# Adding expert outputs in memory by the scatter, and loading small vectors another way

## The chip, the cores and the metric

The kernel runs on one core of a Trainium2 chip. The core has TensorE (PE, matrix products), VectorE (DVE), ScalarE (ACT), GpSimd (POOL) and SyncE (SP, which here only issues DMAs), 16 DMA engines that all queues share, an on-chip memory (SBUF) of 128 partitions and an accumulator memory (PSUM) of 8 banks. The metric is device time in microseconds: 929.48 us, the median of 3 runs from 927.88 to 931.46. The profile is of one further execution.

## What is computed

One layer of a trunk over 256 prompt tokens and 32 sample tokens (288 in all, width 1024), everything in float32. The part before the experts is adaLN modulation from two conditioning vectors, an RMS norm, one input projection, a linear attention with a state, a softmax attention with a cache, an output projection and a second norm. Cut to what matters for the change:

```python
sh1, sc1, gt1, sh2, sc2, gt2 = ada_modulation(c, w_ada, b_ada)     # silu(c) @ w_ada + b_ada, in six parts
h = rms_norm(x, g_mix) * (1.0 + sc1) + sh1
mix, ... = token_mixer(h, ...)                                     # h @ w_in first
x = x + gt1 * mix
h = rms_norm(x, g_ffn) * (1.0 + sc2) + sh2
idx, wts = route(h, w_router, b_router)                            # 8 of 64 experts for each token
routed = sum over the 8 experts e of a token of
         wts * ((silu(h @ w_gate[e]) * (h @ w_up[e])) @ w_down[e])
x = x + gt2 * (routed + shared)
y = rms_norm(x, g_final)
```

So each of 288 tokens gets 8 expert outputs (2304 rows of 4 KB), which must be added.

## The kernel before

All engines run programs written out by hand, with semaphores between them. No scheduler moves anything: the order on an engine is the order in which its block of code is written.

**Head.** SP loads the tokens and eight pieces of `w_ada` of 1 MB (L412, into `ring`), then `w_in` in pieces of 2 MB (into `pair`). PE transposes the tokens, sums their squares (L830) and multiplies the conditioning vectors by the eight pieces (L840). The result stands in PSUM in four pairs of rows. ACT copies them to SBUF (`ada_row`, L491, four copies), PE transposes them (L848, `ada_T`), and DVE makes the modulation (L1255). With it ACT writes the modulated tokens (`hhi`, L507) from the normed ones. ACT also writes the high part of each weight group (`split_hi`, L500, `whi`), DVE the low part (L1274, `wlo`), and from these PE runs the 24 column blocks of the input projection (L870, "z matmuls"). On ACT's own queue, between the norm's square root (L476) and `ada_rows`, stand 12 issues of DMAs: nine small vectors and narrow weights (L479), the cached forget values (`pastf`, L480) and the linear attention's state (L482).

**Expert loop.** A table orders the 64 experts in 32 pairs. A block is up to 64 tokens of each expert of a pair (128 slots on the 128 partitions: expert 0 of the pair on partitions 0 to 63, expert 1 on 64 to 127). A pair mostly takes one block; five further blocks make it 37. The loop's order spreads the pairs with two blocks. In a block PE does the slots' row numbers and weights (L1166), gate and up (L1174), the gather of the next block's tokens (L1150, L1157), and down (L1193). DVE and ACT copy the 128 outputs to `y_slot` (L1607, L641). POOL scatters them (L809): an indirect DMA writes each slot's row of 4 KB to row `rank * 288 + token` of the DRAM tensor `y_d` (eight rows for each token), and empty slots, whose row number lies beyond the bounds, are skipped. POOL waits until it has landed (L812, semaphore `y_gone`). DVE waits for `y_gone` before it computes the next row numbers (`row_f`, L1602, and L1605), and PE waits for these (`row_ok`) at the start of the next block. A scatter issued after one block must therefore have landed before the end of the next. SP loads the weights for the pair after next (L426, `expert_w`, six DMAs of 1 MB each pair): gate and up once PE has read the old ones, down at the end of the pair's last block. PE waits for all six before it starts a block.

**End.** When the last scatter has landed, SP reads `y_d` back: eight loads of 128 KB for the sample tokens (L450) and eight of 1 MB for the prompt tokens (L454) into `y_rank`. The 8 rows of a token are added in part on PE (L1218 with the matrix `four`, L1226 with the identity, accumulating in PSUM) and in part on DVE (L1642 to L1650), which also multiplies by gt2 and adds the rest (`base_tok`, made by ACT at L651). ACT takes the sum of squares and its root (L655, L657), DVE scales (L1629), and SP writes the outputs (L458), in the order sample, first prompt tile, second prompt tile.

Of the kernel before, what the change touches and what calls it, by code (L numbers as in the profile page):

```python
# [53 lines left out]
def layer(nc, x_prompt, x_sample, state_gla, cache_fox_k, cache_fox_v, cache_fox_logf, c_prompt, c_sample,  # L54
# [166 lines left out]
    four = sb("four", [P, NS_])  # L221
# [5 lines left out]
    y_rank = [sb_at(f"y_rank{i}", [P, TOPK, D], F32, RING + 4 * TOPK * D * i) for i in range(3)]  # L227
# [5 lines left out]
    y_d = nc.dram_tensor("y_d", [TOPK * N, D], F32, kind="Internal").ap()  # L233
    gt2_d = nc.dram_tensor("gt2_d", [2, D], F32, kind="Internal").ap()

    def sem(name):
# [8 lines left out]
        "dn_ps acc_ok h2t_ps h2hi_ok h2lo_ok pos_ps rank_ok order_ps table_ok iota_ok rt_zeros sel_ok slots_ps ws_ok row_f_ok row_ok xs_ps xs_ok xg_ps xg_ok pgu_ps sl_ok hid_ok hidT_ps hidT_ok yl_ps yd_ps y_act y_dve y_out y_gone y_rows ys_ps fin_ok sqsum_ok gt2_out tail_in four_ok base_ps base_ok y_sum ssqT_ok rstdT_ok y_ok out_done").split()}  # L245
# [18 lines left out]
    for n, (_, w) in enumerate(pieces):  # L264
        assert w == 1 or at % 2 == 0
        sl = [(at + i) % FRONT for i in range(w)]
        at += w
        waits_of.append(max([owner[q] for q in sl if q in owner], default=-1))
        for q in sl:
            owner[q] = n  # L270
        slots_of.append(sl)
        loads[sl[0]] += 1
        turn.append(loads[sl[0]])
# [6 lines left out]
    def piece_in(eng, n):  # L280

        eng.wait_ge(ring_in[slots_of[n][0]], 16 * turn[n])
# [3 lines left out]

    SHARED = FRONT
# [98 lines left out]
    def ranks_in(i, q):  # L386

        return ring_in[4 * i + q], 16 * (loads[4 * i + q] + PAIRS // 2)
# [10 lines left out]
    def _(sp):  # L399
        for i, (src, tn) in enumerate(((x_prompt[0, 0:128], 128), (x_prompt[0, 128:256], 128), (x_sample[0], 32))):  # L400
            sp.dma_start(x_tok[0:tn, i, :], src).then_inc(s["x_in"], 16)
        for n, (src, w) in enumerate(pieces):
# [9 lines left out]
            sp.dma_start(dst, src).then_inc(ring_in[slots_of[n][0]], 16)  # L412
# [36 lines left out]
        for q in range(TOPK):  # L449
            sp.dma_start(y_rank[2][NS_ * (q % 4):NS_ * (q % 4) + NS_, q // 4, :], y_d[N * q + NP_:N * q + N]).then_inc(ranks_in(2, 0)[0], 16)  # L450
        for i in range(2):
            for q in (2, 3, 0, 1):
                src = y_d.rearrange("(r t) d -> t r d", r=TOPK)[P * i:P * i + P, 2 * q:2 * q + 2, :]
                sp.dma_start(y_rank[i][:, 2 * q:2 * q + 2, :], src).then_inc(ranks_in(i, q)[0], 16)  # L454
        for m, i in enumerate((2, 0, 1)):
            dst = y_sample[0] if i == 2 else y_prompt[0, 128 * i:128 * i + 128]
            sp.wait_ge(s["y_ok"], m + 1)
            sp.dma_start(dst, y_rank[i][0:TN[i], 4, :]).then_inc(s["out_done"], 16)  # L458
# [4 lines left out]
    def _(act):  # L463
# [13 lines left out]
        with nc.allow_non_contiguous_dma(reason="vectors of a few hundred elements"):  # L477
            for dst, src in small[3:]:
                act.dma_start(dst, src).then_inc(s["small_in"], 16)  # L479
        act.dma_start(pastf[:, :, :], cache_fox_logf[0, 0].rearrange("(j p) h -> p j h", p=P)).then_inc(s["cache_in"], 16)  # L480
        for c in range(2):
            act.dma_start(states[:, 4, c, :], state_gla[0, 0, 2 * c:2 * c + 2].rearrange("h k v -> (h k) v")).then_inc(s["state_in"], 16)  # L482

        def ada_rows(r, b):
# [5 lines left out]
            for j in range(4):  # L490
# [4 lines left out]
        def split_hi(g):  # L495

            piece_in(act, FIRST_WIN + g // 2)
# [154 lines left out]
        for m, i in enumerate((2, 0, 1)):  # L652
            n = TN[i]
            act.wait_ge(s["y_sum"], m + 1)
            act.activation(y_rank[i][0:n, 5, :], y_rank[i][0:n, 0, :], ACT.Square, accum_out=ssqT[0:n, i:i + 1]).then_inc(s["ssqT_ok"], 1)  # L655
# [5 lines left out]
    def _(pool):  # L661
# [27 lines left out]
        pool.wait_ge(s["consts"], 1)  # L689
        pool.memset(qA[FD:FD + 2, :, :], 1.0).then_inc(s["ones_ok"], 1)  # L690
# [5 lines left out]
        pool.memset(ada_row[:, :], 0.0).then_inc(s["row_zeros"], 1)  # L696
        pool.wait_ge(s["row_zeros"], 1)
# [86 lines left out]
        pool.tensor_tensor(four[:, :], ident[:, 0:NS_], ident[:, NS_:2 * NS_], ALU.add).then_inc(s["four_ok"], 1)  # L784
        for q in (2, 3):
            pool.wait_ge(s["four_ok"], q - 1)
# [895 lines left out]
```

## Time and profile before

| What | Value |
|---|---|
| Time, median of 3 runs | 929.48 us (927.88 to 931.46) |
| Time of the profiled execution | 932.22 us |
| Its span, first to last instruction | 930.4 us |
| TensorE busy, and its granted clock | 860.4 us (92%), 0.952 of full speed |
| DVE, ACT, POOL busy | 29%, 27%, 10% |
| Read from HBM, written to HBM | 261.34 MB, 22.07 MB |
| Share of 16 DMA engines: SP's queue, POOL's, ACT's | 68.3%, 3.6%, 1.1% |
| Chain that ended last | PE 85%, DVE 5%, DMA 4% |

The page gives shares over the whole span. The three stages that the change touches are the head (0 to 49 us), the expert loop (327 to 883 us) and the end (883 us on). They are read by the chain of waits, which runs back from the last instruction, and by the timeline. A row of the timeline has the start, the duration (of the whole merged run of equal instructions), the engine, the line, and in brackets how long the engine was idle before and what ended that.

### The profile page before, as it was taken

Reading aid. Unit: us, or ns where it says so; the run is one execution under the profiler, and the core shown is the slowest. Engines: PE = TensorE matmul, PEld = TensorE weight load, DVE = VectorE, ACT = ScalarE, POOL = GpSimd, SP = SyncE. Lnnn points to the kernel's source line nnn. Section 1 sums busy time; section 2 is a strip of 40 time slices with the busy share of each in tenths; the row PEclk is TensorE's granted clock in tenths of the full one; section 3 lists DMA queues with packets and bytes.
Section 4 is the critical chain, followed back from the end, with each engine's and each line's share of the span. In section 5 each row is a group of like instructions: output and inputs, shape, how many; then the busy total and the mean of one; then the engine's idle time right before and its main releaser. Section 6 shows DMA issues by size and latency. Waiting matters only on the chain.

```text
span 930.4 us, 13928 instructions
## 1 busy us (share of the span) xinstructions
PE 860.4 (92%) x4436; PEld 470.1 (51%) x4437; DVE 268.6 (29%) x797; ACT 247.9 (27%) x484; POOL 88.4 (10%) x189
## 2 busy tenths in 40 slices
PE   7699999797898999999999999999999999999962
PEld 3199983534686744444444444444444444444521
DVE  2354426435226611111211121121212112121118
ACT  2353424134113312131222212121222213121231
POOL 3000011200022000101101010101101010100000
PEclk9889989798798999999999999999999999999977
DMA  8934447452526369099995999699996999999183
GB/s 326 362 133 160 182 181 276 151 181 92 222 81 263 103 272 376 40 366 415 428 425 245 406 427 426 271 371 420 427 425 254 397 427 426 426 427 426 77 302 157
DMA packets 55370, 273.84 MB, mean 294 GB/s; under 512 B 12720, under 2 KB 13056, under 8 KB 27312
## 3 DMA queue, kind: packets, MB, share of 16 engines
q1 hardware_dynamic: 42064, 258.23, 68.3%
q0 software_dynamic: 6560, 12.55, 3.6%
q10 hardware_dynamic: 6720, 2.70, 1.1%
q8 instruction: 17, 0.28, 0.1%
q14 instruction: 9, 0.07, 0.0%
HBM read 261.34 MB, written 22.07 MB: 305 GB/s over the span
## 4 chain that ended last, share of the span: by engine, by line
PE 85%; DVE 5%; DMA 4%; ACTq 2%; issue 2%; ACT 1%; SPq 0%; POOL 0%; POOLq 0%; DVEq 0%
PE psum L1174 27%; PE psum L1193 13%; PE psum L1150 10%; PE psum L870 8%; PE psum L1157 4%; PE psum L1071 4%; DMA expert_w<-in_w_exp_down 3%; PE psum L840 3%; PE psum L1099 2%; PE psum L1166 2%; PE psum L1089 1%; ACTq L480 1%; PE psum L1183 1%; PE psum L1226 1%; PE psum L825 1%
## 5 line engine op out<-in xcount | busy, mean ns | idle before, releaser
L1174 PE MATMUL psum<-expert_w,xg 128*64 128x512 f32 x1184 | 263.9, 598 | 3.4 <-DMA expert_w<-in_w_exp_down 1.7
L1174 PEld LDWEIGHTS psum<-expert_w,xg 128*64 128x64 f32 x1184 | 85.8, 137 | 150.1 <-issue 149.4
L1193 PE MATMUL psum<-expert_w,hidT 128*64 128x512 f32 x592 | 135.2, 599 | 0.0
L1150 PE MATMUL psum<-h2hl,sel 128*128 128x512 f32 x380 | 97.8, 403 | 0.5 <-ACT acc L616 0.5
L1150 PEld LDWEIGHTS psum<-h2hl,sel 128*128 128x128 f32 x380 | 68.4, 188 | 43.7 <-issue 30.0
L634 ACT ACTIVATE silg<-psum 128x256 f32<-128x256 f32 x37 | 14.2, 384 | 260.9 <-PE psum L1174 260.9
L1193 PEld LDWEIGHTS psum<-expert_w,hidT 128*64 128x64 f32 x592 | 39.3, 137 | 69.6 <-issue 69.6
L1597 DVE SCALAR_TENSOR_TENSOR hid<-psum,ws,silg 128x256 f32<-128x256 f32 x37 | 17.9, 483 | 195.7 <-ACT silg L634 195.7
L623 ACT COPY xs<-psum 128x512 f32<-128x512 f32 x76 | 44.5, 586 | 58.1 <-PE psum L1150 58.1
L1607 DVE COPY y_slot<-psum 128x512 f32<-128x512 f32 x37 | 25.6, 691 | 117.7 <-PE psum L1193 117.7
L1157 PE MATMUL psum<-ident,xs 128*128 128x128 f32 x304 | 47.7, 280 | 0.5 <-ACT xs L623 0.2
L840 PE MATMUL psum<-ring,scT 128*2 128x512 f32 x192 | 46.5, 1091 | 0.3 <-DMA ring<-in_w_ada 0.3
L641 ACT COPY y_slot<-psum 128x512 f32<-128x512 f32 x37 | 21.6, 585 | 93.2 <-PE psum L1193 93.2
L629 ACT COPY xg<-psum 128x512 f32<-128x512 f32 x76 | 40.8, 588 | 18.2 <-PE psum L1157 18.2
L809 POOL DMA_INDIRECT y_d<-y_slot,row x37 | 39.4, 1064 | 19.5 <-issue 19.5
L1580 DVE TENSOR_TENSOR sel<-iota,posm 128x192 fp32r<-128x192 f32 (+1 forms) x76 | 27.9, 367 | 40.9 <-issue 40.9
L1157 PEld LDWEIGHTS psum<-ident,xs 128*128 128x128 f32 x304 | 34.1, 142 | 9.7 <-ACT xs L623 9.5
L1274 DVE TENSOR_TENSOR wlo<-pair,whi 128x2048 fp32r<-128x2048 f32 x12 | 27.5, 2291 | 35.1 <-ACT whi L500 35.1
L1071 PE MATMUL psum<-hT,pair 128*128 128x288 f32 x128 | 33.1, 423 | 0.7 <-issue 0.7
L870 PE MATMUL psum<-hhi,whi 128*128 128x288 f32 x192 | 32.3, 309 | 1.5 <-ACT hhi L507 1.5
L808 POOL TENSOR_TENSOR seen<-zero 1x1 f32<-1x1 f32 x37 | 6.8, 183 | 274.4 <-ACT y_slot L641 274.4
L1071 PEld LDWEIGHTS psum<-hT,pair 128*128 128x128 f32 x128 | 31.8, 315 | 1.7 <-issue 0.8
(370 smaller groups left out, 846.5 us busy)
## 6 DMA issues: line engine op xcount, KB each, us to landing
expert_w<-in_w_exp_gate SPq DMA_DIRECT2D x64, 1024.0 KB, 9.9
expert_w<-in_w_exp_up SPq DMA_DIRECT2D x64, 1024.0 KB, 11.9
expert_w<-in_w_exp_down SPq DMA_DIRECT2D x64, 1024.0 KB, 12.7
ring<-in_w_ada SPq DMA_DIRECT2D x24, 1024.0 KB, 7.0
pair<-in_w_in SPq DMA_DIRECT2D x6, 2048.0 KB, 9.6
y_rank<-y_d SPq DMA_DIRECT2D x8, 1024.0 KB, 12.9
pair<-in_w_out SPq DMA_DIRECT2D x2, 2048.0 KB, 8.2
x_tok<-in_x_prompt SPq DMA_DIRECT2D x2, 512.0 KB, 4.1
```

Of the source, the lines that this page charges most:

```text
L623: act.copy(xs[:, 4 * q:4 * q + 4, :], bank[q][:, :].rearrange("p (k n) -> p k n", k=4)).then_inc(s["xs_ok"], 1)
L629: last = act.copy(xg[:, 4 * q:4 * q + 4, :], bank[q][:, :].rearrange("p (k n) -> p k n", k=4))
L809: pool.indirect_dma_start(y_d[:, :], bass.IndirectOffsetOnAxis(ap=row[:, 0:1], axis=0), y_slot[:, :], None, bounds_check=TOPK * N - 1, oob ...
L840: last = mm(bank[b][32 * j:32 * j + 2, :].rearrange("g (j q) -> g j q", j=4), scT[:, k, :], cols[:, j // 2, 4 * (j % 2):4 * (j % 2) + 4, : ...
L870: last = mm(bank[c % 4][:, 0:N], w[g % 2][:, k, P * q:P * q + P], h[:, k, :], start=k == 0 and w is whi and h is hhi, stop=k == KC - 1 and ...
L1071: last = mm(bank[k % 4][:, 0:N], w, mT[:, j, :], start=j == 0, stop=j == 7)
L1150: last = mm(bank[q][:, :], sel[:, t // 2, :, :], h2hl[:, t, 4 * q:4 * q + 4, :], start=t == 0, stop=t == 4)
L1157: last = tr(bank[q][:, P * k:P * k + P], xs[:, 4 * q + k, :], ident[:, :])
L1174: last = mm(bank[3][CAP * x:CAP * x + CAP, :].rearrange("p (g n) -> p g n", g=2), xg[:, k, CAP * x:CAP * x + CAP], expert_w[2 * u + x][:, ...
L1193: last = mm(bank[4 + half][CAP * x:CAP * x + CAP, :], hidT[:, i, CAP * x:CAP * x + CAP], expert_w[2 * u + x][:, 2, o:o + 512], start=i == ...
L1274: dve.tensor_tensor(wlo[g % 2][:, :, :], half_group(g), whi[g % 2][:, :, :].bitcast(F32), ALU.subtract).then_inc(s["wlo_ok"], 1)
L1580: dve.tensor_tensor(sel[:, :, x, :], iota[:, bass.ds(at, CAP)].unsqueeze(1).broadcast_to([P, 3, CAP]), posm[:, :, bass.ds(e, 1)].broadcast ...
```

## The change

- The scatter adds instead of writing (`compute_op=ALU.add`), and `y_d` has two rows for each token instead of eight: the first expert of a pair adds to row `token`, the second to row `288 + token`, so that no row is named twice in one DMA. The row number no longer needs the rank (a scan on DVE goes, and `beyond` differs by half).
- `y_d` must be zero before: POOL writes 2.36 MB of zeros to it, from the zeroed tile `a_t`, once 8 of the 24 z blocks are done. DVE waits for that before it writes `a_t`.
- At the end SP issues three loads (one for each tile of tokens, both rows of each token) instead of sixteen. PE's additions and the matrix `four` go. DVE does three operations for each tile.
- The nine small loads, `pastf` and the state move from ACT's queue to POOL's, after the memset of `ada_row`, which moves ahead.
- The first rows: of the four copies to `ada_row` in the first round, ACT does two and DVE two. The first piece of `w_in` is loaded in two halves of 1 MB, each on its own semaphore, and the first weight group waits for the first half alone.

```diff
-    y_d = nc.dram_tensor("y_d", [TOPK * N, D], F32, kind="Internal").ap()
+    y_d = nc.dram_tensor("y_d", [2 * N, D], F32, kind="Internal").ap()
...
     @block.sync
+            if n == FIRST_WIN:
+                for q in range(2):
+                    sp.dma_start(dst[:, :, 256 * q:256 * q + 256], src[:, :, 256 * q:256 * q + 256]).then_inc(ring_in[slots_of[n][q]], 16)
...
-        for q in range(TOPK):
-            sp.dma_start(y_rank[2][NS_ * (q % 4):NS_ * (q % 4) + NS_, q // 4, :], y_d[N * q + NP_:N * q + N]).then_inc(ranks_in(2, 0)[0], 16)
-        for i in range(2):
-            for q in (2, 3, 0, 1):
-                src = y_d.rearrange("(r t) d -> t r d", r=TOPK)[P * i:P * i + P, 2 * q:2 * q + 2, :]
-                sp.dma_start(y_rank[i][:, 2 * q:2 * q + 2, :], src).then_inc(ranks_in(i, q)[0], 16)
+        for i in (2, 0, 1):
+            src = y_d.rearrange("(x t) d -> t x d", x=2)[T0[i]:T0[i] + TN[i]]
+            sp.dma_start(y_sum2[i][0:TN[i], 0:2, :], src).then_inc(halves_in(i)[0], 16)
...
     @block.scalar
-            for dst, src in small[3:]:
-                act.dma_start(dst, src).then_inc(s["small_in"], 16)
-        act.dma_start(pastf[:, :, :], ...).then_inc(s["cache_in"], 16)
-        for c in range(2):
-            act.dma_start(states[:, 4, c, :], ...).then_inc(s["state_in"], 16)
...
-            for j in range(4):
+            for j in range(4 if r else 2):
                 act.copy(ada_row[32 * j:32 * j + 2, :], bank[b][32 * j:32 * j + 2, :]).then_inc(s["ada_row"], 1)
...
     @block.gpsimd
+        pool.memset(ada_row[:, :], 0.0).then_inc(s["row_zeros"], 1)
+        pool.wait_ge(s["row_zeros"], 1)
+            for dst, src in small[3:]:
+                pool.dma_start(dst, src).then_inc(s["small_in"], 16)
+            pool.dma_start(pastf[:, :, :], ...).then_inc(s["state_in"], 16)
+        for c in range(2):
+            pool.dma_start(states[:, 4, c, :], ...).then_inc(s["state_in"], 16)
...
+        pool.wait_ge(s["z_ps"], 8)
+        nothing = a_t[:, :, :, :, :].rearrange("p q i c n -> p (q i c n)")
+        pool.dma_start(y_d.rearrange("(p a) d -> p (a d)", a=9).rearrange("p (r n) -> p r n", n=768), nothing[0:64, :].unsqueeze(1).broadcast_to([64, 12, 768])).then_inc(s["y_clear"], 16)
...
             pool.indirect_dma_start(y_d[:, :], bass.IndirectOffsetOnAxis(ap=row[:, 0:1], axis=0), y_slot[:, :], None,
-                                    bounds_check=TOPK * N - 1, oob_is_err=False).then_inc(s["y_out"], 16)
+                                    bounds_check=2 * N - 1, oob_is_err=False, compute_op=ALU.add).then_inc(s["y_out"], 16)
...
     @block.vector
+        dve.wait_ge(s["w_used"], KC)
+        dve.wait_ge(s["row_zeros"], 1)
+        for j in (2, 3):
+            dve.tensor_copy(ada_row[32 * j:32 * j + 2, :], bank[5][32 * j:32 * j + 2, :]).then_inc(s["ada_row"], 1)
...
-        link(dve.tensor_tensor_scan(r_c[:, :], restart[E][:, :], ch[:, :, :].rearrange("p i e -> p (i e)"), 0.0, ALU.mult, ALU.add))
         for n, i in halves:
-            dve.tensor_scalar(w_hl[0:n, i, 3, 0:E], r_c[0:n, :].rearrange("p (i e) -> p i e", i=3)[:, i, :], 17.0, float(N), ALU.subtract, ALU.mult)
+            dve.tensor_scalar(w_hl[0:n, i, 3, 0:E], ch[0:n, i, :], 0.0, -16.0 * N, ALU.mult, ALU.add)
...
-        dve.memset(beyond[:, :], 16.0 * N)
+        for x in range(2):
+            dve.memset(beyond[CAP * x:CAP * x + CAP, :], (16.0 + x) * N)
...
         for m, i in enumerate((2, 0, 1)):
+            dve.wait_ge(halves_in(i)[0], halves_in(i)[1] + 16)
+            link(dve.tensor_tensor(y[0:n, 0, :], y[0:n, 0, :], y[0:n, 1, :], ALU.add))
+            link(dve.tensor_tensor(y[0:n, 0, :], y[0:n, 0, :], gt2B[0:n, 1 if i == 2 else 0, :], ALU.mult))
+            dve.tensor_tensor(y[0:n, 0, :], y[0:n, 0, :], base_tok[0:n, i, :], ALU.add).then_inc(s["y_sum"], 1)
```

The order on ACT in the head, before, from the norm's square root to the first copies of `ada_row`:

```order
L479 DMA b_rt<-in_b_router 128x64
L479 DMA w_gk_69<-in_w_gla_gk 16x256
L479 DMA w_rt<-in_w_router 128x512
L479 DMA w_lf<-in_w_in 128x8x16
L479 DMA w_lf<-in_w_in 128x8x8
L480 DMA pastf<-in_cache_fox_logf 128x4x8
L482 DMA states<-in_state_gla 128x128 x2
L491 COPY ada_row<-psum 2x512 x4
L500 CAST whi_97<-pair_90 128x2048
```

The same place on ACT now (four more of L479's DMAs stood ahead of the rows above):

```order
L476 ACTIVATE sq<-xT 128x288 x8
L479 ACT_TABLE_LOAD
L479 ACTIVATE rstdB<-psum,epst 128x288
L488 COPY ada_row<-psum 2x512 x2
L500 CAST whi_97<-pair_90 128x2048
```

All twelve DMA issues have left this place, and two of the four copies. The DMAs stand on POOL ahead of its memsets of `qA`, `kA` and `a_t`.

The order on DVE at the end, before, for the first two tiles (`y_rank_207` is the sample tile, `y_rank_205` the first prompt tile):

```order
L1637 TENSOR_TENSOR y_rank_207<-psum,gt2B 32x1024
L1638 TENSOR_TENSOR y_rank_207<-y_rank_207,base_tok 32x1024
L1642 TENSOR_TENSOR y_rank_205<-y_rank_205 128x1024
L1644 TENSOR_TENSOR y_rank_205<-psum,y_rank_205 128x1024
L1645 TENSOR_TENSOR y_rank_205<-y_rank_205,gt2B 128x1024
L1646 TENSOR_TENSOR y_rank_205<-y_rank_205,base_tok 128x1024
L1648 TENSOR_TENSOR y_rank_205<-y_rank_205 128x1024
L1649 TENSOR_TENSOR y_rank_205<-y_rank_205,gt2B 128x1024
L1650 TENSOR_TENSOR y_rank_205<-y_rank_205 128x1024
L1628 RECIPROCAL rstdT<-rstdT 32x1
L1629 SCALAR_TENSOR_TENSOR y_rank_207<-y_rank_207,rstdT,g_finB 32x1024
```

The same place now, up to the second prompt tile's last addition:

```order
L1630 TENSOR_TENSOR y_sum_2_206<-y_sum_2_206 32x1024
L1631 TENSOR_TENSOR y_sum_2_206<-y_sum_2_206,gt2B 32x1024
L1632 TENSOR_TENSOR y_sum_2_206<-y_sum_2_206,base_tok 32x1024
L1630 TENSOR_TENSOR y_sum_0_204<-y_sum_0_204 128x1024
L1631 TENSOR_TENSOR y_sum_0_204<-y_sum_0_204,gt2B 128x1024
L1632 TENSOR_TENSOR y_sum_0_204<-y_sum_0_204,base_tok 128x1024
L1622 RECIPROCAL rstdT<-rstdT 32x1
L1623 SCALAR_TENSOR_TENSOR y_sum_2_206<-y_sum_2_206,rstdT,g_finB 32x1024
L1630 TENSOR_TENSOR y_sum_1_205<-y_sum_1_205 128x1024
L1631 TENSOR_TENSOR y_sum_1_205<-y_sum_1_205,gt2B 128x1024
L1632 TENSOR_TENSOR y_sum_1_205<-y_sum_1_205,base_tok 128x1024
```

A prompt tile has three of these operations instead of seven, the sample tile three instead of two, and none reads PSUM.

## Rows read from the trace of the kernel before

**Rows 1.** Timeline, 32 to 43 us: start us, us, engine line op [idle before].
```profile
32.90 2.01 PE L840 MATMUL psum<-ring,scT 128*2 128x512 f32 x8 [0.31 <-DMA ring<-in_w_ada]
...
38.55 2.38 ACT L491 COPY ada_row<-psum 2x512 f32<-2x512 f32 x4 [17.03 <-issue]
...
40.95 1.90 ACT L500 CAST whi<-pair 128x2048 fp32r<-128x2048 f32 x1
...
42.20 0.38 DVE L1255 TENSOR_TENSOR adaT<-psum,b_adaT 128x16 f32<-128x16 f32 x2 [16.11 <-PE psum L848]
```

**Rows 2.** Chain of waits, head and start of the z matmuls: start us, us, what.
```profile
25.28 9.10 ACTq L480
...
40.98 1.13 PE psum L848 x4
...
48.54 77.41 PE psum L870 x568
```

**Rows 3.** Tile expert_w, the two down loads issued at 671.2 and 671.6 us.
```profile
L426 SPq DMA_DIRECT2D expert_w<-in_w_exp_down x2: 333/358/382, 671.2 to 671.6; - x2
...
DMA to landing us min/median/max: 12.2/13.2/14.2
```

**Rows 4.** Chain of waits in the expert loop, two places.
```profile
682.42 3.58 PE psum L1193 x16
...
686.44 7.02 PE psum L1174 x32
...
820.35 16.68 DMA expert_w<-in_w_exp_down
```

**Rows 5.** The page's costliest group: line engine op xcount | busy, mean ns | idle before, releaser.
```profile
L1174 PE MATMUL psum<-expert_w,xg 128*64 128x512 f32 x1184 | 263.9, 598 | 3.4 <-DMA expert_w<-in_w_exp_down 1.7
```

**Rows 6.** Timeline, one scatter in the expert loop, POOL and DVE.
```profile
672.56 1.14 POOL L809 DMA_INDIRECT y_d<-y_slot,row  x1 [0.52 <-issue]
...
680.42 0.18 POOL L812 TENSOR_TENSOR seen<-zero 1x1 f32<-1x1 f32 x1 [6.71 <-DMA y_d<-y_slot,row]
...
680.63 0.33 DVE L1602 TENSOR_REDUCE row_f<-psum 64x1 f32<-64x2 f32 x2 [1.09 <-POOL seen L812]
```

**Rows 7.** Timeline of the end, 883 us on.
```profile
883.56 5.66 ACT L651 COPY base_tok<-psum 128x512 f32<-128x512 f32 x6 [0.42 <-PE psum L1210]
...
886.50 0.18 POOL L812 TENSOR_TENSOR seen<-zero 1x1 f32<-1x1 f32 x1 [1.61 <-DMA y_d<-y_slot,row]
...
886.92 3.59 SPq L450 DMA_DIRECT2D y_rank<-y_d  x8
...
899.74 1.21 DVE L1637 TENSOR_TENSOR y_rank<-psum,gt2B 32x1024 f32<-32x1024 f32 x1 [18.21 <-PE psum L1218]
...
923.12 1.23 DVE L1650 TENSOR_TENSOR y_rank<-y_rank 128x1024 f32<-128x1024 f32 x1
...
926.09 1.28 DVE L1629 SCALAR_TENSOR_TENSOR y_rank<-y_rank,rstdT,g_finB 128x1024 f32<-128x1024 f32 x1
```

**Rows 8.** Tile pair, first load alone: DMA issue and time to landing.
```profile
L412 SPq DMA_DIRECT2D pair<-in_w_in x1: 670/670/670, 27.1 to 27.1; - x1
...
DMA to landing us min/median/max: 11.2/11.2/11.2
```

**Rows 9.** DMA issues by line: count, KB each, median us to landing.
```profile
ring<-in_w_sh_gate SPq DMA_DIRECT2D x1, 1024.0 KB, 4.8
...
y_rank<-y_d SPq DMA_DIRECT2D x8, 128.0 KB, 2.9
```

**Rows 10.** DMA queue of POOL, 604.5 to 697 us: packets, MB, share of 16 engines.
```profile
q0 software_dynamic: 864, 1.18, 3.4%
```

**Rows 11.** The same queue, 500.5 to 593 us.
```profile
q0 software_dynamic: 864, 1.42, 4.0%
```

**Rows 12.** The same queue, 708.5 to 867.7 us.
```profile
q0 software_dynamic: 1440, 2.28, 3.8%
```

**Rows 13.** The same queue, 640 to 656 us.
```profile
q0 software_dynamic: 144, 0.28, 4.5%
```

More of the change, by code:

```diff
@@ L226, in layer @@
     expert_w = [sb_at(f"expert_w{i}", [P, 3, SLOT], F32, RING + 3 * 8192 * i) for i in range(4)]
-    y_rank = [sb_at(f"y_rank{i}", [P, TOPK, D], F32, RING + 4 * TOPK * D * i) for i in range(3)]
+    y_sum2 = [sb_at(f"y_sum2_{i}", [P, 4, D], F32, RING + 4 * 8 * D * i) for i in range(3)]
     psum = nc.alloc_psum_tensor("psum", [P, 8 * 512], F32)
@@ L272, in layer @@
         loads[sl[0]] += 1
+        if n == KC:
+            loads[sl[1]] += 1
         turn.append(loads[sl[0]])
@@ L285, in piece @@
         return ring[slots_of[n][0]] if pieces[n][1] == 1 else pair[slots_of[n][0] // 2]
+    second_turn = 1 + sum(1 for n in range(FIRST_WIN) if slots_of[n][0] == slots_of[FIRST_WIN][1])
     SHARED = FRONT
@@ L384, in y_half, with halves_in @@
         return y[0:TN[i], i, :].rearrange("t (p k) -> t k p", k=KC)[:, 4 * q:4 * q + 4, :]
[L386 to L388 removed]
+    def halves_in(i):
+        return ring_in[4 * i], 16 * (loads[4 * i] + PAIRS // 2)
     def base_bank(i):
@@ L782, in _ @@
         pool.tensor_copy(tok_f[:, :], tok_i[:, :]).then_inc(s["iota_ok"], 1)
-        pool.tensor_tensor(four[:, :], ident[:, 0:NS_], ident[:, NS_:2 * NS_], ALU.add).then_inc(s["four_ok"], 1)
-        for q in (2, 3):
-            pool.wait_ge(s["four_ok"], q - 1)
-            pool.tensor_tensor(four[:, :], four[:, :], ident[:, NS_ * q:NS_ * q + NS_], ALU.add).then_inc(s["four_ok"], 1)
         pool.wait_ge(s["ada_ok"], 3)
@@ L1211, in _ @@
             last.then_inc(s["base_ps"], 1)
-        pe.wait_ge(s["y_act"], num(pe, n))
-        pe.wait_ge(s["y_dve"], num(pe, n))
-        pe.wait_ge(s["four_ok"], 3)
-        pe.wait_ge(ranks_in(2, 0)[0], ranks_in(2, 0)[1] + 16 * TOPK)
-        for half in range(2):
-            for g in range(2):
-                last = mm(bank[4 + half][0:NS_, :], four[:, :], y_rank[2][:, g, 512 * half:512 * half + 512], start=g == 0, stop=g == 1)
-        last.then_inc(s["ys_ps"], 1)
-        for i in range(2):
-            pe.wait_ge(s["base_ok"], 2 * i + 2)
-            for q in range(4, TOPK):
-                if q % 2 == 0:
-                    pe.wait_ge(ranks_in(i, q // 2)[0], ranks_in(i, q // 2)[1] + 16)
-                for half in range(2):
-                    last = mm(bank[base_bank(i) + half][:, :], ident[:, :], y_rank[i][:, q, 512 * half:512 * half + 512], start=q == 4, stop=q == TOPK - 1)
-            last.then_inc(s["ys_ps"], 1)
     @block.vector
```

50 lines of the change are left out of this document (19 added, 31 removed).

## The prediction

> **What bounds the kernel now.** I read the page's shares and its slices first, then the chain of waits from the end back, then the timeline at the three places that the change touches, and last the DMA view of single stretches. The page puts 85% of the chain on PE, so an edit counts only where PE, or what PE waits for, is moved. Three such places matter.
>
> In the head PE ends its products with `w_ada` at 34.9 us and then has nothing to do, though the result is ready: the copies to `ada_row` start at 38.55, after 17 us in which ACT waited for nothing the profile shows [rows 1]. The chain names the cause: one issue on ACT's queue, that of `pastf`, held ACT for 9.10 us from 25.28 [rows 2], and the state's two issues stood behind it. So the reader is to see here an engine blocked by its own DMA queue. After the z matmuls start at 48.54, PE runs through [rows 2]; what is won before them stays won.
>
> In the expert loop PE seems to be the bound, but the DMA engines are as full. The second down load issued at 671.6 takes 14.2 us, to 685.8 [rows 3], and the block that needs it starts at 686.44 [rows 4]: 0.6 us of margin. In the last stretch, without a pair of two blocks, the chain runs through such a load, 16.68 us from 820.35 [rows 4]; over the whole loop PE waits only 1.7 us for these loads [rows 5]. So a little more DMA work in a block comes out as a wait of PE, with the margin as its only cover. A pair of two blocks leaves the DMA engines a block's time to recover.
>
> The scatter has more room. One is issued at 672.56 and seen as landed at 680.42; the row numbers follow in about 0.6 us [rows 6]; PE needs them at 686.0, when its down products end [rows 4]. So a scatter may land 5 us later than now before PE waits for its rows.
>
> At the end, from 886.92 on, SP issues reads of 8 rows for each token. DVE starts at 899.74, and the last scaling ends at 927.4 [rows 7].
>
> **The head.** With no DMA issue before them, the copies start when PE ends, at 34.9. The four took 2.38 us [rows 1], 0.6 each; ACT does two while DVE, idle since its last operation 16 us ago [rows 1], does two. So they end at 34.95 + 1.2 = 36.15 instead of 40.93: 4.8 us earlier. PE's transposes and the modulation follow as before. The second strand is the first weight group: its cast takes 1.90 us and ended at 42.85, together with the modulation [rows 1]. It now needs the first half of the `w_in` piece by 36.15. The whole 2 MB landed at 27.1 + 11.2 = 38.3 [rows 8]. Loads of 128 KB and of 1 MB take 2.9 and 4.8 us [rows 9], so 1 MB costs about 2.1 us, and the first half should land at 36.2 or before, with fewer small loads beside it. I take the whole 4.8 us. Lower bound: if the half, in runs of 1 KB instead of 2 KB, lands no earlier than the whole did, the cast ends at 40.2 and 2.6 us are left. Upper: 0.3 more, if the wait for the last `w_ada` piece [rows 1] goes too. The twelve DMAs move past POOL's memsets of `qA`, `kA` and `a_t`, which nobody needs until after the z matmuls; their first reader is PE after 48.54 + 77.41 = 126 us [rows 2], so POOL's issue time, whatever it is, is covered. If that cover were gone each microsecond would count once.
>
> A rule stands against this. The Trainium skill (DMA: Bandwidth & Descriptors, section Issuing engines are not separate DMA queues) says that issuing from several engines "will only save the time on the sequencer it takes to initiate the DMA, which is usually small relative to the DMA itself". By that rule only the split copies would gain, 1.2 us, and the sum below would be 3.6 us higher. The trace has this time as not small, and I go by it.
>
> **The zeros.** 2.36 MB are written while the z matmuls run; at the 2.1 us for a MB above that is 5 us of the DMA engines in a stage of 77 us. DVE's wait for it stands behind the z matmuls' end. Cost: nothing, as PE covers it. The scan that goes from the routing and the three additions for `four` lie beside PE's shared expert: nothing.
>
> **The end.** The last scatter is seen as landed at 886.50, and SP issues at 886.92 [rows 7]; I give its additions 1 us more, so SP issues at 887.9. The sample tile's 256 KB land 3 us later [rows 9], at 890.9; ACT is done with `base_tok` at 889.2 [rows 7]. DVE does three operations of 1.23 us [rows 7], 3.7 us with their gaps, to 894.6. The first prompt tile's 1 MB has landed by 893.9 (4.8 us and the sample's share); three operations to 898.3; the sample's scaling, about 1.6, to 899.9; the second tile, landed by then, to 903.6. From there to the last scaling's end it was 927.4 - 924.35 = 3.0 us [rows 7], for two scalings and ACT's square and root beside them, and stays so: 906.6. Output and landing took 930.4 - 927.4 = 3.0: 909.6. The end gains 930.4 - 909.6 = 20.8 us. Bounds: 19 (each of the three landings 0.6 late) and 22 (additions at no cost).
>
> **The loop.** Adding in memory must read what stands there. No row shows such a DMA. Bounds: nothing, if the read lies beside the write on the engine; as much engine time again, if an engine's time goes by bytes taken in. I take the second, since the loads, which only take in and put out once, already fill the engines. From 604.5 to 697 the scatters take 3.4% of 92.5 us, 3.15 us for six [rows 10]; from 500.5 to 593, 4.0%, 3.7 us [rows 11]; the first stretch, near 396 to 478, is like their mean, 3.4. In each, the loads of the last of the six blocks fall before a pair of two blocks and have a block's time to spare, so five of six count: 5/6 * (3.15 + 3.7 + 3.4) = 8.5 us. Off that go the margins, 0.6 us each by the one case [rows 3, 4]: 1.8. In the last stretch all ten count and no margin is left: 3.8% of 159.2 = 6.05 us [rows 12]. Sum 8.5 - 1.8 + 6.05 = 12.8 us more. The scatter itself, 0.7 us of engine time now [rows 13], stays far inside its 5 us.
>
> **The sum.** 930.4 - 4.8 - 20.8 + 12.8 = 917.6 us of span. The execution's span stood 0.9 above the median of the runs (929.48), so the time is 916.7 us.
>
> **Rivals.** *The read is hidden.* The additions cost the DMA engines nothing: 930.4 - 25.6 - 0.9 = 903.9 us. For it: an engine takes in and puts out at once. Against: the full slices of the loop have no spare room that a row shows.
>
> *The fullest engine decides* (slower). A load is complete only when the last of the 16 engines has done its part. A scatter's 128 slots are 8 to an engine; if one engine has 8 full ones, it does 8 more reads. In one scatter 0.28 MB, 68 rows, took 4.5% of 16 us on 16 engines [rows 13]: 0.72 us, or 0.17 us a row on its engine. Eight rows are 1.35 us a block, and 15 + 10 blocks count: 33.9 - 1.8 = 32.1 us. Time: 930.4 - 25.6 + 32.1 - 0.9 = 936.0. It turns to a loss from (25.6 + 1.8) / 25 = 1.1 us a block. Against it: now, too, the fullest engine carries the writes, and the margin above lasts through a stretch all the same.
>
> *Each row's read is waited for.* If the engine stands still between a row's read and its write, the scatter takes far longer. Were its 7.9 us from issue to landing [rows 6] doubled, to 15.8, it would miss its 12.9 us by 2.9 in each of some 35 blocks: 930.4 - 25.6 + 100 - 0.9 = 1004 us. The Trainium skill (DMA: Bandwidth & Descriptors, section Latency and other measured facts) gives 0.2 us for an HBM access on average and 2 us at high load. As an estimate from that page, 3.6 rows on an engine at 0.2 us would add 0.7 us a block, some 934 us in all; at 2 us it would be far above 1004. No row shows such an addition.
>
> *The head does not do what it says:* the first half of `w_in`, or the small loads now among the `w_ada` pieces, hold it up, and half the gain or all is lost: 919 to 922.
>
> **How the numbers follow.** Main case 0.50 (its own range 909 to 926), hidden read 0.17, head without gain 0.10, fullest engine 0.15, waited read 0.08. The time is that of the main case, 916.7. The range 902 to 945 leaves out the waited read and the outer tails of two others, under 2 in 10. A difference of 0.5%, 4.6 us, is about what a measurement of this kernel can tell: faster means under 924.8, slower over 934.1. Faster: most of the main case, the hidden read, most of the head's case: 0.67. Slower: two thirds of the fullest engine's case, the waited read, a tail of the main: 0.20. Same: 0.13.
>
> **What would show it.** Head: the copies to `ada_row` start near 35 us and the z matmuls' long run begins near 43.7. If the cast (`whi`) starts late, the half load is to blame. Loop: PE's blocks keep their length where DMA has margin; the wait before L1174 on `expert_w` grows from 1.7 us to some 14; POOL's queue has twice its share of the engines in the same stretch. If a scatter's landing goes over 13 us, `row_f` and PE's row products wait, and the forecast is wrong upwards. If PE's waits stay near 2 us, the read was hidden. End: DVE's three operations a tile run without waits on DMA, and the last scaling ends some 20 us after the last scatter is seen. The forecast falls if the queue's share grows threefold or more.

## The result, and the profile after

The changed kernel takes 926.36 us (median of 16 runs, 923.27 to 929.75). The kernel before, run beside it on the same chip, takes 931.69 us (16 runs, 927.88 to 933.77). The ratio is 0.9947, with a 95% interval of 0.9933 to 0.9961: 0.5% faster, where 1.4% was forecast. The profiled execution took 926.23 us, with a span of 924.2.

The span fell by 6.2 us. Cut at the loop's first product with a gate matrix and at its last down product, which both kernels have, it splits like this:

| stage | before, us | after, us | measured | forecast |
|---|---|---|---|---|
| start to the loop | 327.5 | 323.1 | -4.4 | -4.8 |
| expert loop | 555.0 | 573.0 | +18.0 | +12.8 |
| last down product to the end | 47.9 | 28.1 | -19.8 | -20.8 |

**Head.** The timeline of the changed kernel, 32 to 43 us (columns as in [rows 1]):

```profile
32.46 2.01 PE L844 MATMUL psum<-ring,scT 128*2 128x512 f32 x8 [0.33 <-DMA ring<-in_w_ada]
34.54 1.18 ACT L488 COPY ada_row<-psum 2x512 f32<-2x512 f32 x2 [13.48 <-PE psum L844]
34.54 1.42 DVE L1255 COPY ada_row<-psum 2x512 f32<-2x512 f32 x2 [8.91 <-PE psum L844]
35.74 1.90 ACT L500 CAST whi<-pair 128x2048 fp32r<-128x2048 f32 x1
...
36.77 0.38 DVE L1244 TENSOR_TENSOR adaT<-psum,b_adaT 128x16 f32<-128x16 f32 x2 [0.82 <-PE psum L852]
```

The copies now start when PE's products end, at 34.54, instead of 3.6 us after them [rows 1]. ACT's idle time before them ends with PE, no longer with "issue". The cast starts right behind the copies, so the first half of `w_in` was there. In the chain of waits the long run of z matmuls begins 5.4 us earlier than in [rows 2], and its end comes 5.0 us earlier:

```profile
43.11 77.87 PE psum L874 x568
```

**Loop.** The page's costliest group, the line of POOL's DMA, and POOL's queue over the whole kernel:

```profile
q0 software_dynamic: 7392, 15.49, 8.3%
...
L1179 PE MATMUL psum<-expert_w,xg 128*64 128x512 f32 x1184 | 265.6, 601 | 19.0 <-DMA expert_w<-in_w_exp_down 10.4
...
L813 POOL DMA_INDIRECT y_d<-y_slot,row x37 | 60.7, 1640 | 19.7 <-issue 19.7
```

Before, PE's idle time ahead of these products was 3.4 us [rows 5]; it is 19.0 now, of which the profile names the down loads for 10.4. The same stretch as in [rows 12], 708.5 to 867.7 us (other blocks fall into it by a few microseconds):

```profile
q0 software_dynamic: 1440, 2.61, 9.1%
```

The share went from 3.8% to 9.1% for 2.61 MB instead of 2.28: per MB 2.1 times as much. The chain of waits in the last stretch shows where it is paid (start us, us, what):

```profile
782.90 7.09 PE psum L1179 x32
...
797.89 16.79 DMA expert_w<-in_w_exp_down
814.67 0.24 issue
814.91 7.09 PE psum L1179 x32
...
829.89 19.33 DMA expert_w<-in_w_exp_down
849.22 0.24 issue
849.46 7.09 PE psum L1179 x32
...
864.43 16.90 DMA expert_w<-in_w_exp_down
```

PE's products start two blocks apart in these rows: 32.0 us from 782.90 to 814.91, 34.55 us to 849.46. Two blocks of PE's own work are 29.7. So PE follows the down loads' landings. The two scatters issued within the longer step have 107 and 89 rows (their 4 KB packets in the trace); those on either side of them have 64 rows or fewer. That the steps are so uneven is what the experiments follow up.

The scatter itself never held anything up. One of the loop, in the timeline of POOL and DVE (compare [rows 6]):

```profile
676.07 1.71 POOL L813 DMA_INDIRECT y_d<-y_slot,row  x1 [0.52 <-issue]
685.11 0.18 POOL L816 TENSOR_TENSOR seen<-zero 1x1 f32<-1x1 f32 x1 [7.33 <-DMA y_d<-y_slot,row]
...
685.33 0.33 DVE L1595 TENSOR_REDUCE row_f<-psum 64x1 f32<-64x2 f32 x2 [0.97 <-POOL seen L816]
```

From issue to seen it takes 9.0 us instead of 7.9 [rows 6]; the longest of all landed in 11.0 us.

**End.** The timeline from the last scatter on (compare [rows 7]):

```profile
897.50 1.55 POOL L813 DMA_INDIRECT y_d<-y_slot,row  x1 [0.52 <-issue]
901.99 0.18 POOL L816 TENSOR_TENSOR seen<-zero 1x1 f32<-1x1 f32 x1 [2.94 <-DMA y_d<-y_slot,row]
...
902.40 1.32 SPq L457 DMA_DIRECT2D y_sum<-y_d  x3
...
905.72 1.21 DVE L1630 TENSOR_TENSOR y_sum<-y_sum 32x1024 f32<-32x1024 f32 x1 [10.62 <-DMA y_sum<-y_d]
...
919.85 1.28 DVE L1623 SCALAR_TENSOR_TENSOR y_sum<-y_sum,rstdT,g_finB 128x1024 f32<-128x1024 f32 x1
```

From the scatter's landing seen to the last scaling's end it was 40.9 us [rows 7] and is 19.1 now; after its first operation DVE waits for no DMA. The last scatter, with 8 rows and nothing beside it on the DMA engines, lands 4.4 us after its issue instead of 2.5.

### The profile page after: what moved, and what is told of

It is laid out like the page before. It is cut to its first block, busy times and chain, and to the rows that moved or that the text cites. A ratio compares the mean times of both kernels' runs of the same rounds, so it can differ in the third digit from the quotient of the medians.

```text
span 924.2 us, 13840 instructions
## 1 busy us (share of the span) xinstructions
PE 842.7 (91%) x4396; PEld 467.4 (51%) x4397; DVE 261.7 (28%) x792; ACT 246.8 (27%) x482; POOL 117.3 (13%) x199
## 4 chain that ended last, share of the span: by engine, by line
PE 76%; DMA 15%; DVE 5%; issue 2%; ACT 1%; SPq 0%; POOL 0%; POOLq 0%; DVEq 0%; ACTq 0%
PE psum L1179 23%; DMA expert_w<-in_w_exp_down 13%; PE psum L1198 11%; PE psum L874 8%; PE psum L1155 8%; PE psum L844 4%; PE psum L1162 4%; PE psum L1076 4%; PE psum L1104 2%; PE psum L1171 1%; PE psum L1094 1%; DMA ring<-in_w_ada 1%; PE psum L829 1%; PE psum L1086 1%; PE psum L1065 1%
## 5 line engine op out<-in xcount | busy, mean ns | idle before, releaser
L1179 PE MATMUL psum<-expert_w,xg 128*64 128x512 f32 x1184 | 265.6, 601 | 19.0 <-DMA expert_w<-in_w_exp_down 10.4
L1179 PEld LDWEIGHTS psum<-expert_w,xg 128*64 128x64 f32 x1184 | 90.6, 138 | 163.4 <-issue 163.0
L813 POOL DMA_INDIRECT y_d<-y_slot,row x37 | 60.7, 1640 | 19.7 <-issue 19.7
L816 POOL TENSOR_TENSOR seen<-zero 1x1 f32<-1x1 f32 x37 | 6.8, 183 | 269.6 <-DMA y_d<-y_slot,row 269.6
L1573 DVE TENSOR_TENSOR sel<-iota,posm 128x192 fp32r<-128x192 f32 (+1 forms) x76 | 27.8, 366 | 41.0 <-issue 41.0
L812 POOL TENSOR_TENSOR seen<-zero 1x1 f32<-1x1 f32 x37 | 6.8, 183 | 234.0 <-ACT y_slot L641 234.0
```

The lines of the kernel that those rows point to most:

```text
L813: pool.indirect_dma_start(y_d[:, :], bass.IndirectOffsetOnAxis(ap=row[:, 0:1], axis=0), y_slot[:, :], None, bounds_check=2 * N - 1, oob_is ...
L1179: last = mm(bank[3][CAP * x:CAP * x + CAP, :].rearrange("p (g n) -> p g n", g=2), xg[:, k, CAP * x:CAP * x + CAP], expert_w[2 * u + x][:, ...
L1573: dve.tensor_tensor(sel[:, :, x, :], iota[:, bass.ds(at, CAP)].unsqueeze(1).broadcast_to([P, 3, CAP]), posm[:, :, bass.ds(e, 1)].broadcast ...
```

## The experiments

All ratios are against the kernel before, run on the same chip (its medians there: 930.43 us beside e1, e2, e4 and e5, 931.41 beside e3, e6, e7 and e8, 931.36 beside e9 to e11). Loop and end are cut as above. "Landing distance" is the time between the last landings of two neighbouring blocks' down loads, where the loads have no block to spare, read from each load's landing in the trace. A block's rows are those that its scatter moves, counted as its 4 KB packets.

**e1: writes in place of additions.** The expert outputs of a token's four experts overwrite each other; their sums are left out.

```diff
-                oob_is_err=False, compute_op=ALU.add)
+                oob_is_err=False)
```

> The changed kernel with the scatter writing its rows instead of adding them, still to two rows for each token; the sums are left out. Theory 'the read costs engine time': the loop (first gate product to last down product) goes from 573.0 us back to about 555, and the last scatter from 4.4 us to 2.5, so the span falls from 924.2 to 904 to 906 and the time to some 2.7% below the kernel before. Rival 'something else in the changed kernel slows the loop' (zeros, row placement in two rows only): the loop stays over 565 us and the time near 926.

Measured: 904.99 us, ratio 0.973 (0.9701 to 0.9759). The loop takes 555.7 us, the landing distances in the last stretch are 15.4 us (one of 14.88), and 15.97 and 16.0 for the blocks of 107 and 89 rows, nearly as in the kernel before (15.38 and 15.95). Its page:

```profile
q0 software_dynamic: 7392, 15.48, 5.3%
...
L1179 PE MATMUL psum<-expert_w,xg 128*64 128x512 f32 x1184 | 263.9, 598 | 4.0 <-DMA expert_w<-in_w_exp_down 1.9
...
L813 POOL DMA_INDIRECT y_d<-y_slot,row x37 | 39.4, 1065 | 19.5 <-issue 19.5
```

The packet count is the changed kernel's and PE's idle time is back at 4.0 us: the whole 17 us of the loop are the additions' doing, not those of two destination rows. POOL's issue, too, is shorter by 0.6 us without them. Against e2 below, which has the old end, it is 21 us shorter: that is what the new end is worth.

**e2: the head's edits alone**, in the kernel before (loads on POOL's queue, two copies on DVE, `w_in`'s first piece in halves).

> The kernel before with the edits of the head alone (small loads on POOL, two copies on DVE, first piece of w_in in halves). Theory: z matmuls start 5.4 us earlier, 4.4 to 5 us are left at the end, time 4 to 5 us (0.5%) under the kernel before. Rival 'the head's gain is given back in the loop, where the DMA is full': under 2 us.

Measured: 926.37 us, ratio 0.9948 (0.9928 to 0.9969). The z matmuls' long run starts at 43.68 instead of 48.54, and its end comes 3.6 us early. The ratio is worth 4.8 us, the difference of the medians 4.1: the head gives about what was forecast, and the loop (554.3 us) gives none of it back.

**e3: no rows moved.** Every slot of the changed kernel gets a row number beyond the bounds, so the scatters are issued and leave all expert outputs out.

```diff
-            dve.memset(beyond[CAP * x:CAP * x + CAP, :], (16.0 + x) * N)
+            dve.memset(beyond[CAP * x:CAP * x + CAP, :], 40.0 * N)
```

> The changed kernel, with every slot's row number beyond the bounds, so that the scatters are issued and move no row (the expert outputs are left out of the result). Theory (a block's loads take a base plus so much for each row on the scatter's fullest engine): with no rows only the base is left. From the two kinds of block seen so far the base works out at 14.75 us, so the down loads land 14.7 to 14.9 us apart in the last stretch, the loop takes 551 to 553 us (555.7 with plain writes, 573.0 with additions) and the kernel about 902 us. Rival (the scatter's issue and its 128 descriptors cost the loads something whether or not a row is moved): landings stay 15.4 apart, the loop at 555 or more, 905 or more. Second rival (the base is really the weights' own rate and the writes cost nothing): landings 15.4 apart as well, so a value under 15 speaks for the theory alone.

Measured: 902.03 us, ratio 0.9681 (0.9645 to 0.9717); loop 551.2 us, landing distances 14.71 to 14.83 us in the middle of every stretch (15.1 to 15.3 at the ends of the last one). Two rows of its page:

```profile
L1179 PE MATMUL psum<-expert_w,xg 128*64 128x512 f32 x1184 | 263.9, 598 | 0.1
...
L813 POOL DMA_INDIRECT y_d<-y_slot,row x37 | 60.7, 1639 | 19.7 <-issue 19.7
```

PE does not wait at all. The loads alone take 14.77 us a block, less than PE's 14.9, and POOL's long issue, still 1639 ns, costs the loop nothing. So everything above 14.77 comes from rows moved.

**e4 and e5: the same rows and bytes, other slots.** The experts' outputs stand in slots, one to a partition, 64 to each of two experts. An expert with 30 tokens fills slots 0 to 29. Both kernels change only which position of an expert's list goes to which slot: e4 deals them over runs of four partitions in turn, e5 fills eight neighbouring positions into two runs of four that are 32 partitions apart.

```diff
-        pool.iota(iota_i[:, :], pattern=[[1, MAXB * CAP]], base=0, channel_multiplier=0)
+        pool.iota(iota_i[:, :].rearrange("p (h e l) -> p h e l", e=8, l=4),
+                  pattern=[[32, 2 * MAXB], [1, 8], [8, 4]], base=0, channel_multiplier=0)
```

for e4, and for e5

```diff
+        pool.iota(iota_i[:, :].rearrange("p (j h e l) -> p j h e l", h=2, e=8, l=4),
+                  pattern=[[64, MAXB], [4, 2], [8, 8], [1, 4]], base=0, channel_multiplier=0)
```

(the plain numbers that the table of experts takes from the same tile come from a copy made before)

> The changed kernel with the slots of an expert laid out otherwise on the partitions: slot s of a half goes to the (s mod 8)th run of four partitions (and its copy 32 further on), so that n rows are at most ceil(n/8) on any DMA engine, if an engine serves partitions 4e to 4e+3 and 32+4e to 35+4e of a half. Theory 'the fullest engine decides, and engines serve such runs of four': the loads' landings come 15.1 to 15.8 us apart where they now come 16.0 apart (4 rows on the fullest) and 17.3 (8 rows), the loop falls from 573.0 to about 561 us, the time to about 914. Rival 'the mean over the engines decides': no change. Rival 'an engine serves eight partitions in a row': slower or no change in small blocks.

> The changed kernel with the opposite layout: slots 8e to 8e+7 of a half all on the two runs of four partitions of engine e, so that every block with 8 rows or more in a half has 8 on its fullest engine. Theory 'the fullest engine decides': landings 17.3 us apart in nearly every block, the loop at about 590 us, the time at about 945. Rival 'the mean decides': no change (926).

Measured: e4 914.93 us, ratio 0.9822 (0.9792 to 0.9851), loop 563.2; e5 949.56 us, ratio 1.0206 (1.0173 to 1.0239), loop 597.2. Of e4's page and of e5's:

```profile
q0 software_dynamic: 7392, 15.49, 8.3%
...
L1185 PE MATMUL psum<-expert_w,xg 128*64 128x512 f32 x1184 | 263.9, 598 | 10.8 <-DMA expert_w<-in_w_exp_down 6.0
```

```profile
q0 software_dynamic: 7392, 15.49, 7.9%
...
L1185 PE MATMUL psum<-expert_w,xg 128*64 128x512 f32 x1184 | 280.0, 628 | 28.6 <-DMA expert_w<-in_w_exp_down 26.7
```

The queue's packets and bytes are equal and its share is even lower in e5 (of a longer span), and yet 35 us lie between them, 34 of them in the loop. A mean share can't tell them apart; the fullest engine can. The landing distances against the number of rows on the fullest engine, if an engine serves runs of four partitions, 32 apart, and a block's rows are split evenly between its two experts:

| kernel | rows on the fullest engine | landing distance, us | 14.77 + rows * price |
|---|---|---|---|
| e3 | 0 | 14.71 to 14.83 | 14.77 |
| before, e1 (written, 0.159 a row) | 4 | 15.38 | 15.41 |
| before, e1, two blocks | 8 | 15.95, 15.97 | 16.04 |
| after (added, 0.327 a row) | 4 | 16.03 | 16.08 |
| after, two blocks | 8 | 17.25 to 17.3 | 17.39 |
| e4, blocks of 80, 59, 41, 31 rows | 5, 4, 3, 2 | 16.34, 16.05, 15.72, 15.35 | 16.41, 16.08, 15.75, 15.42 |
| e5, nearly all | 8 | 17.1 to 17.7 | 17.39 |
| e5, the block of 11 rows | 6 | 16.67 | 16.73 |

The prices are the median durations of the 4 KB packets on POOL's queue in the traces, 159 ns where rows are written and 327 where they are added; they are not fitted. That rows in all don't count shows best in the kernel before: its last stretch has blocks of 11, 33, 45 and 64 rows, all with four on the fullest engine, and all land 15.37 to 15.41 us apart. Six of the eight distances in e4's last stretch stand off by about one row: its blocks of 107 and 89 rows take 16.69 and 16.36 us, where 7 and 6 rows would make 17.06 and 16.73, and those of 66, 33, 11 and 43 rows are 0.25 to 0.4 us short too. It is not their size: in e9 below, with the same slots, the blocks of 107, 89 and 43 rows take 17.00, 16.63 and 15.73 us, as worked out (17.06, 16.73, 15.75). Why that stretch is shorter stays open.

**e6 and e7: pairs of two blocks later.** The last stretch without such a pair is twelve blocks long in the changed kernel. e6 turns the order of the six turns around, so that it has six; e7 has e4's slots as well.

```diff
-                  pattern=[[2, turns], [2 * turns, SPREAD], [1, 2]], base=EARLY, channel_multiplier=0)
+                  pattern=[[2, turns], [-2 * turns, SPREAD], [1, 2]], base=EARLY + 2 * turns * (SPREAD - 1), channel_multiplier=0)
```

> The changed kernel with the order of the table's turns reversed, so that the last stretch without a pair of two blocks holds six blocks and not twelve; the same blocks, rows and bytes. Theory (additions cost only where the loads have no block's time to spare; five of six blocks count in a short stretch, all of them in the last): about 12 us less, 912 to 917 us; the last stretch's part of the loop's excess goes. Rival (the additions cost the same wherever they stand, since the bytes are the same): 925 to 928 us.

> The changed kernel with both: slots dealt over the 16 engines in turn (914.9 alone) and the turns reversed. Theory: the two overlap, since both take from the same waits for down loads: the loop takes 551 to 555 us (573.0 in the changed kernel, 563.2 with the slots dealt alone), 901 to 908 us in all. If they add up in full (11.4 and 12 us) 902 to 903. Rival (order does nothing, only the deal): 914 to 916.

Measured: e6 921.42 us, ratio 0.9903 (0.9867 to 0.994), loop 565.3; e7 909.16 us, ratio 0.9751 (0.9723 to 0.9779), loop 556.8. e6 gave some 4 to 5 us instead of 12 (the loop 7.7): the blocks of 103 and more rows now come in the first stretch, where PE's blocks grow to as much as 17.5 us (in the changed kernel the first seven are not held up), and the kernel ends with a block of 107 rows, whose scatter takes 6.1 us and not 4.4. e7 misses its range by 1 us, in the same two places: its first stretch has PE blocks of up to 16.6 us, and its end takes 29.7. It is still the fastest kernel here that computes everything:

```profile
L1185 PE MATMUL psum<-expert_w,xg 128*64 128x512 f32 x1184 | 265.6, 601 | 3.6 <-DMA expert_w<-in_w_exp_down 2.5
```

**e8: e4's slots in the kernel before.**

> The kernel before with the slots dealt over the 16 engines in turn. Theory (a written row costs 0.159 us on its engine, half of an added one, and the loads have almost kept up with PE): landings in the last stretch fall from 15.4 to about 15.1 us, only 1 to 2 us of waits for loads are there to be saved, so the time is 0.997 to 1.000 of before. Rival (dealing the slots does something else that helps, such as shorter routing or a shorter end, and e4's gain was that): as in e4 against the changed kernel, 0.988.

Measured: 927.89 us, ratio 0.9964 (0.9943 to 0.9985), landing distances 15.51, 15.37, 15.22 and 15.05 us for 80, 59, 41 and 31 rows (worked out with 0.159: 15.57, 15.41, 15.25, 15.09). The size is a little more than expected; its loop is 1.6 us shorter and its end 0.9, with a last scatter of 2.2 us instead of 2.5. The deal by itself brings no more than that, so e4's gain did not come from somewhere else.

**e9: the turn without a pair first**, with e4's slots, for a last block of 31 rows.

```diff
-                  pattern=[[2, turns], [2 * turns, SPREAD], [1, 2]], base=EARLY, channel_multiplier=0)
+                  pattern=[[-2, turns], [2 * turns, SPREAD], [1, 2]], base=EARLY + 2 * (turns - 1), channel_multiplier=0)
```

> The changed kernel with the slots dealt over the engines and, unlike e7, only the turn without a pair of two blocks moved to the front: stretches of 7, 7, 7, 7 and 6 blocks between such pairs, and a last block of 31 rows, so that the last scatter is as short as in the changed kernel (e7's took 6.0 us, e4's 3.1). Theory (waits for loads by the fullest engine; the end starts when the last scatter has landed): the loop 556 to 559 us (556.8 in e7), the end 26.7 to 28 (29.7 in e7), so about 906 to 910 us, level with e7 or 2 us better. Rival (e7's shorter loop came from its order by size, not from where the pairs stand): the loop at 563, 914 us.

Measured: 914.09 us, ratio 0.9815 (0.9776 to 0.9855), loop 562.4, end 27.8. The end came as expected, the loop did not: blocks of 107 and 89 rows now stand at the front, where PE's blocks take up to 16.8 us, and as much as the last stretch gained is lost there. The time is the rival's: level with e4 (914.93 us), so moving this turn gained nothing. Where the pairs stand is not all; which blocks stand between them counts too.

**e10 and e11: the head in two parts**, each in the kernel before. e10 moves the small loads alone:

```diff
-            for dst, src in small[3:]:
-                act.dma_start(dst, src).then_inc(s["small_in"], 16)
+            for dst, src in small[3:]:
+                pool.dma_start(dst, src).then_inc(s["small_in"], 16)
```

(and the past gates and the state likewise). e11 has the two copies on DVE and the halves of `w_in`:

```diff
-            for j in range(4):
+            for j in range(4 if r else 2):
...
+            if n == FIRST_WIN:
+                for q in range(2):
+                    sp.dma_start(dst[:, :, 256 * q:256 * q + 256], src[:, :, 256 * q:256 * q + 256]).then_inc(ring_in[slots_of[n][q]], 16)
```

> The kernel before with one edit of the head alone: the small vectors, the past gates and the state issued on POOL's queue instead of ACT's; the four copies to ada_row stay on ACT and w_in's first piece stays whole. Theory (ACT was held by its own queue): the copies start at 34.6 to 35 us instead of 38.55 and end at 37.3; the cast whi then waits for the whole piece, landing at about 37.6, and ends near 39.5 instead of 42.85, so the z matmuls begin some 3.3 us earlier: about 0.9965 of before. Rival (an issue is short beside its transfer, the copies waited for something else): they start at 38.5 as before and the time is 1.000.

> The kernel before with the other edits of the head: two of the four copies on DVE, w_in's first piece in two halves; the small loads stay on ACT's queue. Theory: ACT is still held until 38.55, does two copies by 39.75 and starts the cast then, 1.2 us earlier than before (40.95); the z matmuls begin 1.2 us earlier, 0.999 of before. Rival (the halves or the split are what gave the 5 us): the whole 5 us, 0.995.

Measured: e10 929.81 us, ratio 0.998 (0.9958 to 1.0002); e11 926.01 us, ratio 0.9948 (0.993 to 0.9965). In e10 the copies start at 34.71, as the theory had it, and the z matmuls' end comes 4.0 us early, though the medians show only 1.6 us, with an interval from nothing to 3.9. So the rows bear the theory out against its rival; the time alone would not. e11 went against its theory: 5 us and not 1.2. Its timeline on ACT:

```profile
25.70 7.34 ACTq L487 DMA_DIRECT2D pastf<-in_cache_fox_logf  x1
33.07 2.14 ACTq L489 DMA_DIRECT2D states<-in_state_gla  x2
35.45 1.18 ACT L498 COPY ada_row<-psum 2x512 f32<-2x512 f32 x2 [13.61 <-PE psum L850]
```

The same two issues that held ACT until 38.45 before [rows 1, 2] are done by 35.21, in time for PE's end. e8, with the head unchanged, shows 38.64 for the copies again, so this is the edit and hardly chance. The split copies stand behind these issues and can't have shortened them. That leaves the cut of `w_in`'s piece into two loads on SP's queue: with it ACT's queue let go sooner. Why, no run here shows, and the halves were not run alone. The same load of `pastf` takes 0.78 us to issue from POOL's queue at 11.3 us in e10 and in the changed kernel. So either edit takes most of the stall. At the z matmuls' end e10 is 4.0 us early, e11 3.7, and both together 3.6 (e2) to 5.0 (the changed kernel): they overlap and don't add.

## Why the prediction was wrong

The sign and the three places were right, the size was not: 916.7 forecast, 926.36 measured, with its 5 us of gain where 13 were expected.

- **The head** (-4.8) held: -5.4 at the long run, -4.4 at the loop, and e2's ratio is worth 4.8 (its medians 4.1). The halves landed in time, the issue on POOL was covered. The reason given, that ACT was held by its own queue, is what the rows show, and e10 confirms where the copies start. But the split copies were priced at 1.2 us by themselves, and e11 shows that with the halves they are worth most of the whole (3.7 us at the z matmuls' end), since ACT's queue then let go earlier, which the prediction did not see.
- The Trainium skill's rule (DMA: Bandwidth & Descriptors, section Issuing engines are not separate DMA queues), that the time to issue is usually small beside the DMA, did not hold for `pastf` on ACT's queue, whose issue took 9.10 us [rows 2] of 20.8 to its landing, and 7.34 in e11; from POOL's queue, at 0.78 of 9.7 us in e10, it did. The forecast that followed it, 1.2 us for the head, would have been out by 3.6.
- **The end** (-20.8) held within 1 us: -19.8. The last scatter's additions cost 1.9 us there instead of the 1 allowed.
- **The loop** (+12.8) was the step that failed, at +18.0, and in it one term: the price of the additions, taken as "as much engine time again" on the scatters' mean share of the 16 engines. The doubling was right, 159 to 327 ns a row. What was wrong was to take the mean. It gave 0.57 us a block (3.4 us for six) and 0.6 in the last stretch. A load lands when its slowest part has, so the engine with the most rows counts: 4 rows * 0.168 = 0.67 us a block, also where the block has only 33 rows, and 1.35 where eight rows stand on one engine.
- **What that makes of the sum.** An estimate from each block's rows: over the 25 blocks that the forecast counts, the fullest engine has some 82 rows in the three short stretches and 53 in the last, which at 0.168 us are 13.8 and 8.9 us, 22.7 in all, where the mean gave 8.5 and 6.05. By the starts of PE's blocks the three short stretches lost 10.2 us and the last 7.8. So the margins covered some 4.7 us and not the 1.8 allowed: a second error, which hid a part of the first. The loads had been half a microsecond a block slower than PE (15.4 against 14.86 us) and now are 1.2 slower, so what a pair of two blocks leaves to spare is used up sooner: in each short stretch only the last three blocks grew, and in the last one the first two did not grow at all and seven of the later ones by 0.7 to 1.4 us each.
- **The rival of the fullest engine** had the right mechanism, and the right price for a row (0.17). It took eight rows in every block, before and after. It was dismissed because the fullest engine "carries the writes" before as well: true, and no objection, since the doubling falls on it too. Eight rows nearly everywhere is e5, at 949.6 us and not 936.0, because the kernel before has four in most blocks and not eight.
- **The read hidden:** refuted by e1, which lies 21 us under the changed kernel. **Each row's read waited for:** refuted, the scatters land within 11.0 us.
- **What should have shown it.** Of the signs named, the wait ahead of L1174 (L1179 after) went from 1.7 to 10.4 us by the profile's name for it, where some 14 were forecast, and from 3.4 to 19.0 us as idle time in all; the queue's share went to twice and a little more. Both read as "more of the same mechanism". The real sign stood in the trace of before: the landing distance of 15.38 us, and 15.95 for two blocks (read only after the result), which a mean over 16 engines can't explain.

## What to carry to other kernels

Beside weight loads that fill the DMA engines, price a scatter by the rows on its fullest engine, not by bytes or mean share, and deal its live rows over the engines before you count on the rest: here the deal alone was worth 11 us. Additions in memory cost twice the engine time of writes, so they pay where the DMA engines stand idle, and are to be weighed where loads are late; in this kernel they took back 17 of the 24 us that the head and the end had won (e1). When an engine waits on its own DMA issues, look at what the other queues carry at that time before you decide which edit frees it.

## What the runs showed of the hardware that was not expected

- A row of 4 KB that is added takes its DMA engine 327 ns, one that is written 159 ns. The issue of the scatter takes POOL 1.64 us instead of 1.06, also when no row is moved (e3).
- An indirect scatter's rows go to an engine by their partition in runs of four, 32 apart: the deal by that rule gained 11 us (e4), packing by it cost 23 (e5). The Trainium skill (DMA: Bandwidth & Descriptors, section The descriptor swizzle) has this split for one direct transfer of 1 MiB to 128 partitions; here the landing distances follow it for a scatter whose rows go wherever their tokens are.
- The z matmuls' end and the loop's start lie 199.1 us apart in e11 and 203.7 in e10, with the same instructions between them; PE's granted clock there is 0.90 and 0.87 of full speed, and its busy time 173.0 and 177.7 us. The traces of the other kernels fall in the same order: 199.0 to 199.5 us at a clock of 0.89 or 0.90, 201.5 to 202.2 at 0.87 (201.5 before, 202.1 in the changed kernel). So up to 4.7 us of what a head edit seems to gain or lose can be this clock, and e10 and e11 are best compared at the z matmuls' end.
- Where PE waited most, its products were slower too: in e5 L1185 took 628 ns instead of 598, and the granted clock (the third number from the end: PEclk) was 0.95 of 2.4 GHz on average from 835 to 867 us: PE waited 2.46 us for a load, began its products at 852.26, and from 852.4 to 855.8 the clock stood at 0.5, which is 1.2 GHz. The kernel before has 1.00 from 835 to 867 us. The row of e5, of the busy times by stretch:

```profile
835.00:867.00 32.00, 29.53 (x133) 13.91 (x134) 4.85 (x21) 6.39 (x13) 4.04 (x6) 0.95 1.00 380
```
